# Where the second RMSNorm's scale is applied in a hybrid attention layer on one Trainium2 core

## Chip, core and metric

The kernel runs on one NeuronCore of a Trainium2 chip. Its engines run beside each other and meet only at semaphores: PE (TensorE, products into PSUM), DVE (VectorE), ACT (ScalarE), POOL (GpSimd) and SP (SyncE, which issues the loads). The metric is the device time of one execution in microseconds (us). All times below are us unless ns stands there.

## What is computed

One inference step of a one-layer encoder over 1024 prompt tokens and 64 sample tokens, 1088 columns in all, with 1024 channels. After the two attention branches comes the part that matters here:

```
x  = x + gt1 * einsum(merged, w_out)                      # output projection
h2 = rms_norm(x, g_norm2) * (1.0 + sc2) + sh2             # second norm, scale and shift per channel
u  = relu(einsum(h2, w_up))                               # 1024 -> 4096
x  = x + gt2 * einsum(u * u, w_down)                      # 4096 -> 1024
rms_norm(x, g) = x / sqrt(mean over channels of x*x + EPS) * g
```

gt1, sc2, sh2 and gt2 come from a conditioning vector: one value per channel for the prompt and one for the sample tokens. They lie in modT; gain2 is g_norm2 * (1 + sc2).

## The kernel before

Everything is kept transposed: channels in the partitions (KT = 8 tiles of 128), tokens in the columns. xT is x, 8 tiles of 1088 columns. A product with a float32 weight tile is made in three products of a rounded format: the high part of the weights with the high part of the data, high with low, low with high. So each operand is split into hi and lo: hi is a copy into the rounded type, lo the difference.

A job is one weight tile of 128 x 1024, loaded by SP into w_raw, split by POOL into w_hi (L724) and w_lo (L726), in two slots. POOL starts a split once PE has begun the job before it (w_used, L795) and the data has landed. PE runs group_product (L781) for three groups of 364, 362 and 362 columns (GROUPS, L35), each 8 channel tiles times three products, 24 in all, into a PSUM bank of its own; six banks are used in turn, and PE waits (bank_free, L786) until DVE has evicted the group six before. All three groups of a job use the same weights.

The output projection (L1162) is eight jobs, one for each tile m of xT. DVE adds each group, times gt1, to xT (add_scaled, L1881, L1892); ACT squares the finished tile into sq_tmp (L1457), DVE adds that to sq_sum (L1904). These are loops of four turns over two tiles.

Then comes the norm. PE waits for sq_sum and for all banks (L1170 to L1172), sums over the channels with nine pairs of products against a column of ones, tokens in the partitions (L1175). DVE makes the mean, ACT the root, DVE the reciprocal, of nine columns (L1909 to L1914). PE spreads the result over 128 partitions with nine pairs of products (L1182) into banks 5 to 7. Then for each of eight tiles: DVE multiplies xT by it (h2_n, L1927), ACT applies gain2 and the shift in two pieces, prompt and sample (h2_f, L1467), and copies to h2_hi (L1471), and the difference h2_lo is made by DVE for even tiles (L1919) and by POOL for odd ones (L769). The split of the first up job stands before these on POOL's queue, the second behind them.

The feed-forward is a loop of eight passes (L1191). A pass is four up jobs (d = 0 to 3) and four down jobs. In the very first group PE waits for h2_hi and h2_lo tile by tile (h2_ready, L1186). Each up group is evicted by DVE with relu (L1937), squared by ACT (L1479), copied to u_hi (L1481), and DVE makes u_lo (L1942), which waits for ACT before DVE goes to the next group. The first three groups of the down product wait for the last u_lo's (L1202). Down groups are added to xT by add_scaled (L1948). After the loop the final norm and the stores follow.

## Time and profile before

| | |
|---|---|
| median of 3 runs | 1935.29 (1929.22 to 1940.74) |
| the profiled execution: time | 1928.07 |
| its span, first to last instruction | 1926.3 |
| mean granted TensorE clock | 0.972 |
| output projection, last product starts | 1093.68 |
| first up job starts its second group | 1133.21 |
| second up job starts | 1142.21 |
| passes of the feed-forward | 8, from about 1132 to 1901 |

The profile is of one execution. Its first part gives busy time by engine. The chain of waits follows the work that ended last back from the end. The timeline gives instructions in order of time, with the idle time of their engine before them in brackets and what ended it; "x2" is two instructions merged in a row. The windows give busy time and the granted clock in a stretch, as a share of 2.4 GHz. The groups by form give count, total and mean duration of instructions of one line and shape. The trace names tiles by prefix: h_hi and h_lo stand for h2_hi and h2_lo there, h_n and h_f for h2_n and h2_f.

### The profile page before, as it was taken

The numbers are of one execution on the slowest core, as the hardware profiler recorded it, in microseconds if no ns is written. First come the engines' busy times: TensorE is split into PE (matmuls) and PEld (weight loads), VectorE is DVE, ScalarE is ACT, GpSimd is POOL, SyncE is SP. The second block draws the span as 40 slices with busy tenths as digits, with TensorE's granted clock in tenths as the row PEclk, the third lists the DMA queues.
The fourth block names the chain that finished last, engine by engine and source line by source line (L and its number), as shares of the span: only waits on it lengthen the run. The fifth ranks groups of instructions, "written<-read, shape, count | busy, mean of one in ns | idle before, by whom it ended". The sixth has DMA issues, their size and how long they took to land.

```text
span 1926.3 us, 30314 instructions
## 1 busy us (share of the span) xinstructions
PE 1811.3 (94%) x11206; PEld 1718.9 (89%) x11206; DVE 978.2 (51%) x2263; ACT 584.7 (30%) x1115; POOL 473.9 (25%) x273
## 2 busy tenths in 40 slices
PE   7599999999978898999999869999999999999996
PEld 2498999999978887778999869999999999999996
DVE  1547888899145556555653344343434343434344
ACT  3345566641244444443320151111111111111112
POOL 0331222224210100120323132222222222222220
PEclk9699999999989998999999979999999999999998
DMA  7420124242442223653443101111111111111112
GB/s 269 136 61 23 57 90 112 91 127 79 125 108 69 58 57 91 181 154 124 136 138 99 33 22 45 44 44 44 44 44 44 44 44 44 44 44 44 44 44 93
DMA packets 179317, 153.40 MB, mean 80 GB/s; under 512 B 20240, under 2 KB 162016, under 8 KB 178688
## 3 DMA queue, kind: packets, MB, share of 16 engines
q1 hardware_dynamic: 175328, 137.31, 24.8%
q10 hardware_dynamic: 3920, 15.19, 2.0%
q8 instruction: 42, 0.69, 0.2%
q14 instruction: 27, 0.22, 0.0%
HBM read 127.34 MB, written 25.19 MB: 79 GB/s over the span
## 4 chain that ended last, share of the span: by engine, by line
PE 83%; DVE 7%; ACT 5%; DMA 2%; issue 2%; POOL 1%; SPq 0%; DVEq 0%; ACTq 0%; POOLq 0%
PE psum L791 65%; PE psum L1066 4%; PE psum L1057 2%; PE psum L915 2%; PE psum L1084 2%; PE psum L948 2%; PE psum L829 1%; PE psum L1029 1%; PE psum L1030 1%; DVE u_lo L1942 1%; DVE h_f L1559 1%; PE psum L1033 1%; DVE logit L1754 1%; DMA out<-y_out 1%; DVE score L1616 1%
## 5 line engine op out<-in xcount | busy, mean ns | idle before, releaser
L791 PE MATMUL psum<-h_hi,w_hi 128*128 128x362 f32 (+1 forms) x1440 | 477.6, 332 | 17.5 <-POOL h_lo L769 10.7
L791 PE MATMUL psum<-h_lo,w_hi 128*128 128x362 f32 (+1 forms) x1440 | 475.6, 330 | 0.0
L791 PE MATMUL psum<-h_hi,w_lo 128*128 128x362 f32 (+1 forms) x1440 | 474.7, 330 | 0.0
L724 POOL CAST w_hi<-w_raw 128x1024 fp32r<-128x1024 f32 x112 | 124.5, 1112 | 1020.4 <-PEq L795 825.0
L791 PEld LDWEIGHTS psum<-h_hi,w_hi 128*128 128x128 f32 x1440 | 272.6, 189 | 21.4 <-POOL h_lo L769 12.6
L726 POOL TENSOR_TENSOR w_lo<-w_raw,w_hi 128x1024 fp32r<-128x1024 f32 x112 | 275.9, 2464 | 9.0
L1892 DVE SCALAR_TENSOR_TENSOR xT<-psum,modT,xT 128x64 f32<-128x64 f32 (+7 forms) x288 | 136.3, 497 | 275.3 <-PE psum L791 275.3
L791 PEld LDWEIGHTS psum<-h_hi,w_lo 128*128 128x128 f32 x1440 | 273.1, 190 | 0.0
L791 PEld LDWEIGHTS psum<-h_lo,w_hi 128*128 128x128 f32 x1440 | 273.0, 190 | 0.0
L791 PE MATMUL psum<-u_hi,w_hi 128*128 128x362 f32 (+1 forms) x768 | 253.2, 330 | 2.7 <-DVE u_lo L1942 2.7
L791 PE MATMUL psum<-u_lo,w_hi 128*128 128x362 f32 (+1 forms) x768 | 252.4, 329 | 0.0
L791 PE MATMUL psum<-u_hi,w_lo 128*128 128x362 f32 (+1 forms) x768 | 251.7, 328 | 0.0
L1479 ACT ACTIVATE u_sq<-u_relu 128x362 f32<-128x362 f32 (+1 forms) x96 | 48.8, 508 | 623.5 <-DVE u_relu L1937 623.5
L1942 DVE TENSOR_TENSOR u_lo<-u_sq,u_hi 128x362 fp32r<-128x362 f32 (+1 forms) x96 | 114.5, 1193 | 107.0 <-ACT u_hi L1481 107.0
L791 PEld LDWEIGHTS psum<-u_hi,w_hi 128*128 128x128 f32 x768 | 144.3, 188 | 5.1 <-issue 5.1
L791 PEld LDWEIGHTS psum<-u_hi,w_lo 128*128 128x128 f32 x768 | 144.7, 188 | 0.0
L791 PEld LDWEIGHTS psum<-u_lo,w_hi 128*128 128x128 f32 x768 | 144.5, 188 | 0.0
L1637 DVE TENSOR_SCALAR_CACHE_REDUCE count_dump<-score,thresh 128x384 f32<-128x384 f32 (+4 forms) x160 | 130.6, 876 | 1.1
L1937 DVE TENSOR_SCALAR u_relu<-psum 128x362 f32<-128x362 f32 (+1 forms) x96 | 51.2, 533 | 142.4 <-PE psum L791 142.4
L752 POOL TENSOR_TENSOR q_hl<-q_raw,q_hl 64x1088 fp32r<-64x1088 f32 x16 | 39.9, 2494 | 309.7 <-ACT q_hl L1372 285.7
L1292 ACT ACTIVATE sign_dump<-score,thresh 128x1024 f32<-128x1024 f32 x64 | 102.2, 1600 | 20.5 <-DVE thresh L1633 20.5
L1066 PEld LDWEIGHTS psum<-kv_tok,probT 128*128 128x128 f32 (+1 forms) x584 | 71.8, 196 | 18.4 <-issue 16.8
(286 smaller groups left out, 2813.8 us busy)
## 6 DMA issues: line engine op xcount, KB each, us to landing
w_raw<-in_w_in SPq DMA_DIRECT2D x32, 512.0 KB, 4.1
ada_c<-in_w_ada SPq DMA_DIRECT2D x32, 512.0 KB, 4.1
w_raw<-in_w_up SPq DMA_DIRECT2D x32, 512.0 KB, 4.0
w_raw<-in_w_down SPq DMA_DIRECT2D x32, 512.0 KB, 3.5
zT_scratch<-z_out ACTq DMA_DIRECT2D x27, 544.0 KB, 2.7
q_raw<-zT_scratch SPq DMA_DIRECT2D x32, 272.0 KB, 5.1
gate<-zT_scratch SPq DMA_DIRECT2D x16, 544.0 KB, 4.5
ada_w<-in_w_ada SPq DMA_DIRECT2D x4, 2048.0 KB, 9.6
```

Of the source, the lines that this page charges most:

```text
L724: pl.tensor_copy(w_hi[slot][:, :], w_raw[slot][:, :]).then_inc(sem("w_hi_made"), 1)
L726: pl.tensor_tensor(w_lo[slot][:, :], w_raw[slot][:, :], w_hi[slot][:, :].bitcast(F32), ALU.subtract).then_inc(sem("w_split"), 1)
L752: pl.tensor_tensor(q[64:P, :], q_raw[64:P, ::-1], q[64:P, :].bitcast(F32), ALU.subtract)\
L791: ins = pe.matmul(bank(b, n), w[:, k, wc], x[:, a, c0:c0 + n], start=(m == 0 and p == 0), stop=(m == len(wk) - 1 and p == 2))
L915: ins = pe.matmul(bank(4 + g, m), w[slot][:, k * P:k * P + P], x[:, k, c0:c0 + m], start=(k == 0 and p == 0), stop=(k == KT - 1 and p == 2))
L1066: ins = pe.matmul(bank(6 + u["n"] % 2)[:, HD * lane:HD * lane + HD], probT[s][0:n, m * P:m * P + P], values(u, kb), start=(kb == 0), stop= ...
L1292: ins = ac.activation(sign_dump[g % 2][r, 0:c.stop - c.start], score[r, c], ACT.Sign, scale=-1.0, bias=thresh[r, g:g + 1].bitcast(F32), ac ...
L1479: ac.activation(u_sq[:, s, 0:n], u_relu[:, s, 0:n], ACT.Square).then_inc(sem("u_squared"), 1)
L1637: return dv.tensor_scalar(count_dump[r, c], score[r, c], th[r, g:g + 1].bitcast(F32), None, op, ALU.add, accum_out=count[r, g:g + 1])
L1892: ins = dv.scalar_tensor_tensor(x, ps if isinstance(m, int) else ps.unsqueeze(1), gt, x, ALU.mult, ALU.add)
L1937: dv.tensor_scalar(u_relu[:, s, 0:n], bank(3 * (d % 2) + g, n), 0.0, None, ALU.max)\
L1942: dv.tensor_tensor(u_lo[:, d, c0:c0 + n], u_sq[:, s, 0:n], u_hi[:, d, c0:c0 + n].bitcast(F32), ALU.subtract).then_inc(sem("u_done"), 1)
```

## The change

h2 = rstd * (gain2 * x) + shift, and rstd is a number per token, so it can be applied after the product over channels: W_up h2 = rstd * (W_up (gain2 x)) + W_up shift. The changed kernel does this.

- In the output projection, ACT makes h2_hi of tile m as a copy of xT times gain2, in two pieces, and DVE makes h2_lo as xT times gain2 minus h2_hi, in two pieces, right after the tile's last group is evicted. The square and the sum follow. The loops are written out over eight tiles.
- h2_hi and h2_lo get two more columns at the front, the shifts of the prompt and of the sample. The up product runs over 1090 columns in groups of 366, 362 and 362 (UP_GROUPS). The two extra results are copied to b_up at the eviction.
- The norm's small steps and the pass over eight tiles go. In their place, after the second group of the first up job, three fp32 products of a 128x128 block of ones with sq_sum, over 512, 512 and 64 columns (spread_mean), give the sum in all partitions at once; the third waits until DVE has read both before it. DVE makes the mean, ACT the root, DVE the reciprocal of all 1088 columns (rstd_b).
- At the eviction of an up group DVE multiplies by rstd_b; ACT applies relu with b_up as bias (two pieces in the third group, where prompt and sample meet), then square and copy. DVE makes u_lo of a group behind the eviction of the next.
- POOL only splits weights. The first pass of the feed-forward is written out, and a loop of seven follows.

```diff
+UP_GROUPS = [(0, 366), (366, 362), (728, 362)]
+MEAN_PARTS = [(0, 512), (512, 512), (1024, 64)]
...
-        h2_hi = at("h2_hi", [P, KT, TOK], F32R, A)
-        h2_lo = at("h2_lo", [P, KT, TOK], F32R, A + ACTW)
+        h2_hi = at("h2_hi", [P, KT, TOK + 2], F32R, A)
+        h2_lo = at("h2_lo", [P, KT, TOK + 2], F32R, A + KT * (TOK + 2))
...
@@ GpSimd
-            split(0)
-            for k in range(1, KT, 2):
-                pl.wait_ge(sem("h2_hi_done"), k + 1)
-                pl.tensor_tensor(h2_lo[:, k, :], h2_f[:, k % 2, :], h2_hi[:, k, :].bitcast(F32), ALU.subtract)\
-                    .then_inc(sem("h2_done1"), 1)
-            for d in range(1, 8):
-                split(d % 2)
-            splits(7, 8)
+            splits(8, 8)
...
@@ TensorE
+            def spread_mean():
+
+                pe.wait_ge(sem("sq_added"), 1 + KT)
+                pe.wait_ge(sem("ones_ready"), 1)
+                for m, (c0, n) in enumerate(MEAN_PARTS):
+                    if m == 2:
+                        pe.wait_ge(sem("sq_mean"), 2)
+                    pe.matmul(bank(6 + m % 2, n), ones[:, :], sq_sum[:, c0:c0 + n], start=True, stop=True)\
+                        .then_inc(sem("sq_spread"), 1)
 
             def h2_ready(k):
-                pe.wait_ge(sem(f"h2_done{k % 2}"), k // 2 + 1)
+                pe.wait_ge(sem("h2_lo_done"), k + 2)
...
+                    for g, (c0, n) in enumerate(UP_GROUPS):
                         group_product(d % 2, KT, range(KT), slice(0, P), h2_hi, h2_lo, range(KT), c0, n, 3 * (d % 2) + g,
-                                      first=(g == 0), ready=h2_ready if d == 0 and g == 0 else None)
+                                      first=(g == 0), ready=h2_ready if first and d == 0 and g == 0 else None)
+                        if first and d == 0 and g == 1:
+                            spread_mean()
...
@@ ScalarE
+            for m in range(KT):
+                ac.wait_ge(sem("bank_free"), sums.next(3))
...
+                ac.activation(h2_hi[:, m, 2:2 + SEQ], xT[:, m, 0:SEQ], ACT.Copy, scale=gain2[:, m, 0:1])
+                ac.activation(h2_hi[:, m, 2 + SEQ:2 + TOK], xT[:, m, SEQ:TOK], ACT.Copy, scale=gain2[:, m, 1:2])\
+                    .then_inc(sem("h2_hi_done"), 1)
+                ac.wait_ge(sem("sq_added"), m + 1)
+                ac.activation(sq_tmp[:, :], xT[:, m, :], ACT.Square).then_inc(sem("squared"), 1)
...
-                        ac.wait_ge(sem("u_relu_done"), us.next())
+                        ac.wait_ge(sem("u_scaled"), us.next())
+                        for a, w, smp in seq_spans(g):
+                            x = u_relu[:, s, a - c0:a - c0 + w]
+                            ins = ac.activation(x, x, ACT.Relu, bias=b_up[:, d % 2, smp:smp + 1])
+                        ins.then_inc(sem("u_relu_done"), 1)
+                        ac.wait_ge(sem("u_relu_done"), us.n)
...
@@ VectorE
+                dv.wait_ge(sem("h2_hi_done"), m + 2)
+                dv.scalar_tensor_tensor(h2_lo[:, m, 2:2 + SEQ], xT[:, m, 0:SEQ], gain2[:, m, 0:1],
+                                        h2_hi[:, m, 2:2 + SEQ].bitcast(F32), ALU.mult, ALU.subtract)
...
+            for m, (c0, n) in enumerate(MEAN_PARTS):
+                dv.wait_ge(sem("sq_spread"), m + 1)
+                dv.tensor_scalar(rstd_b[:, c0:c0 + n], bank(6 + m % 2, n), 1.0 / DM, EPS, ALU.mult, ALU.add).then_inc(sem("sq_mean"), 1)
+            for m, (c0, n) in enumerate(MEAN_PARTS):
+                dv.wait_ge(sem("sq_root"), m + 1)
+                ins = dv.reciprocal(rstd_b[:, c0:c0 + n], rstd_b[:, c0:c0 + n])
...
-                        dv.tensor_scalar(u_relu[:, s, 0:n], bank(3 * (d % 2) + g, n), 0.0, None, ALU.max)\
-                            .then_inc(sem("u_relu_done"), 1)
...
+                        if g == 0:
+                            dv.tensor_copy(b_up[:, d % 2, :], ps[:, 0:2])
+                            ps = ps[:, 2:n + 2]
+                        dv.tensor_tensor(u_relu[:, k % 2, 0:n], ps, rstd_b[:, c0:c0 + n], ALU.mult).then_inc(sem("u_scaled"), 1)
+                        dv.wait_ge(sem("u_scaled"), relus.n + (k + 1))
                         dv.sem_inc(sem("bank_free"), 1)
+                        if k:
+                            u_low(k - 1)
+                u_low(11)
```

## Rows read from the trace of the kernel before

**Rows 1.** The page's first part: engine, busy us (share), instructions.

```profile
PE 1811.3 (94%) x11206; PEld 1718.9 (89%) x11206; DVE 978.2 (51%) x2263; ACT 584.7 (30%) x1115; POOL 473.9 (25%) x273
```

**Rows 2.** The chain of waits, 1097 to 1178: start, us, what.

```profile
1097.90 3.52 PE psum L1175 x18
1102.30 4.41 PE psum L1182 x18
...
1132.14 46.13 PE psum L791 x267
```

**Rows 3.** Timeline at the output projection's end: start, us, engine, line, instruction [idle before].

```profile
1093.68 0.32 PE L791 MATMUL psum<-m_hi,w_lo 128*128 128x362 f32 x1
1094.16 0.72 DVE L1892 SCALAR_TENSOR_TENSOR xT<-psum,modT,xT 128x298 f32 x2 [3.40 <-PE psum L791]
1095.08 1.11 ACT L1457 ACTIVATE sq_tmp<-xT 128x1088 f32 x1 [10.83 <-DVE xT L1892]
...
1096.31 1.29 DVE L1904 TENSOR_TENSOR sq_sum<-sq_sum,sq_tmp 128x1088 f32<-128x1088 f32 x1 [1.43 <-ACT sq_tmp L1457]
```

**Rows 4.** Timeline where the second up job starts, and POOL's next cast.

```profile
1142.21 0.33 PE L791 MATMUL psum<-h_hi,w_hi 128*128 128x364 f32 x1
...
1142.63 1.04 POOL L724 CAST w_hi<-w_raw 128x1024 fp32r<-128x1024 f32 x1 [7.10 <-issue]
1143.75 2.40 POOL L726 TENSOR_TENSOR w_lo<-w_raw,w_hi 128x1024 fp32r<-128x1024 f32 x1
1154.59 1.04 POOL L724 CAST w_hi<-w_raw 128x1024 fp32r<-128x1024 f32 x1 [8.44 <-issue]
```

**Rows 5.** Windows: stretch, us, busy by engine, granted clock, DMA share, GB/s.

```profile
1134.00:1136.00 2.00, 2.00 (x9) 2.00 (x8) 0.81 (x1) 1.01 (x2) 1.52 (x1) 0.54 0.00 0
```

**Rows 6.** Timeline: a sum begun inside POOL's w_lo, and ACT's two-piece scale.

```profile
1083.42 2.41 POOL L726 TENSOR_TENSOR w_lo<-w_raw,w_hi 128x1024 fp32r<-128x1024 f32 x1
1084.37 2.61 DVE L1904 TENSOR_TENSOR sq_sum<-sq_sum,sq_tmp 128x1088 f32<-128x1088 f32 x1 [1.44 <-ACT sq_tmp L1457]
...
1108.06 1.57 ACT L1467 ACTIVATE h_f<-h_n,modT,gain 128x1024 f32<-128x1024 f32 x2 [6.07 <-DVE h_n L1927]
```

**Rows 7.** Timeline of PE at the kernel's start: eight fp32 products of 512 columns.

```profile
29.23 7.03 PE L829 MATMUL psum<-ada_w,siluT 128*2 128x512 f32 x16
```

**Rows 8.** Timelines by engine where a pass turns from up to down.

```profile
1274.53 0.54 DVE L1937 TENSOR_SCALAR u_relu<-psum 128x362 f32<-128x362 f32 x1 [1.81 <-PE psum L791]
1276.17 2.50 DVE L1942 TENSOR_TENSOR u_lo<-u_sq,u_hi 128x362 fp32r<-128x362 f32 x1 [1.11 <-ACT u_hi L1481]
...
1275.64 0.51 ACT L1481 ACTIVATE u_hi<-u_sq 128x362 fp32r<-128x362 f32 x1
...
1275.87 2.41 POOL L726 TENSOR_TENSOR w_lo<-w_raw,w_hi 128x1024 fp32r<-128x1024 f32 x1
...
1278.80 0.43 PE L791 MATMUL psum<-u_hi,w_hi 128*128 128x362 f32 x1 [0.34 <-DVE u_lo L1942]
```

**Rows 9.** Groups by form, DVE's reciprocals: count | busy us, mean ns | idle before.

```profile
L1725 DVE RECIPROCAL rden<-rsum 128x1 f32<-128x1 f32 x36 | 5.7, 158 | 0.0
...
L1913 DVE RECIPROCAL mid_rstd<-mid_rstd 128x8 f32<-128x8 f32 x1 | 0.2, 202 | 0.4 <-ACT mid_rstd L1461 0.4
...
L1914 DVE RECIPROCAL mid_rstd<-mid_rstd 64x1 f32<-64x1 f32 x1 | 0.1, 103 | 0.0
```

**Rows 10.** Two gaps of PE in the attention part, and the windows around them.

```profile
537.11 0.77 PE L1057 MATMUL psum<-ident,logit 128*128 128x128 f32 x5 [2.41 <-ACT logit L1380]
...
605.92 0.55 PE L1057 MATMUL psum<-ident,logit 128*128 128x128 f32 x3 [1.59 <-DVE yA_lo L1789]
...
536.00:540.00 4.00, 2.89 (x15) 2.67 (x16) 1.05 (x2) 2.18 (x6) 0.73 (x3) 0.81 0.93 222
540.00:544.00 4.00, 4.00 (x24) 3.78 (x23) 2.32 (x7) 2.00 (x4) 0.00 (x0) 0.76 0.97 210
...
604.00:608.00 4.00, 2.41 (x23) 2.17 (x21) 2.00 (x8) 1.64 (x4) 0.00 (x0) 1.00 0.02 4
```

134 lines of the change are left out of this document (49 added, 85 removed).

## The prediction, made before the changed kernel was run

> **What bounds the kernel now.** I read the page's totals first: TensorE (PE) is busy 94% of the span [rows 1], so only a stretch where PE is not dense can give time back. The chain of waits names the one in reach [rows 2]: PE runs densely until 1094.0, then the chain passes through the two fp32 PE steps of the mean (L1175, L1182), VectorE (DVE), ScalarE (ACT) and GpSimd (POOL), and PE is dense again only from 1132.14. The timeline gives the ends: the last product of the output projection starts at 1093.68 and lasts 0.32 [rows 3]; the second job of the up product starts at 1142.21 [rows 4]. Between these lie three groups of 24 products. Jobs of three groups recur every 11.96 us (the casts of w_hi at 1142.63 and 1154.59, [rows 4]), or 0.166 us a product. So 1142.21 - 1094.01 = 48.2 us are spent on 12.0 us of work: the norm costs 36.2 us. Part of it is the clock: PE was idle from 1094.0 to 1097.9, and at 1134 it still ran mostly at the lower of its two levels, 1.2 GHz (0.54 granted, [rows 5]).
>
> **What goes.** Everything between the last eviction and the first up product: 3.5 us and 4.4 us of PE [rows 2], the small DVE and ACT steps, and eight tiles of h2_n, h2_f, h2_hi, h2_lo. POOL's share of h2_lo, every second tile, goes with them.
>
> **What stays on the path: tile 7.** Tiles 0 to 6 are split behind earlier products. The last tile is complete only with the eviction that starts at 1094.16 and takes 0.72 [rows 3]. ACT then makes h2_hi in two pieces, 1024 and 64 columns; the nearest row is the same pair with a bias, 1.57 together [rows 6]. Before, ACT started its square at 1095.08 [rows 3], so h2_hi is ready near 1095.08 + 1.57 = 1096.65. DVE then subtracts, both inputs in SBUF. Such a subtraction or sum takes 1.29 for 1088 columns when alone [rows 3], but 2.61 when it starts inside POOL's w_lo: started 1084.37, POOL busy 1083.42 to 1085.83, done 1086.98, 1.15 after POOL [rows 6]. Will POOL be there? It splits a job's weights once PE has begun the job before: cast 0.42 after the start, w_lo 1.12 later, 2.40 long [rows 4]. With the up product starting at 1094.05 that is 1095.6 to 1098.0, over the 1096.65. So h2_lo is ready at 1098.0 + 1.3 = 1099.3 (two pieces). PE meanwhile does 21 products of group 0, to 1094.05 + 21 x 0.166 = 1097.5, waits 1.8 us, and finishes the group with three at 1099.9. Bounds of this wait: 0.6 if POOL doesn't hold DVE, 3 if ACT and DVE are slower by 1.2 together. Group 1 ends at 1103.9.
>
> **Added on PE: the spread mean.** Three fp32 products with a 128x128 block of ones, 512, 512 and 64 columns. Nothing like it is in the trace. The nearest is 512 columns with two weight columns: 16 instructions, two to a product, in 7.03 us, 0.88 each product [rows 7]; a load of 128 fp32 weight columns adds a little, so I take 1.0. The third must wait until DVE has read the second: an eviction of 362 columns takes 0.54 [rows 8], so 0.7 for 512, with 0.3 for two hand-overs. Third product 0.3. Sum 1.0 + 1.0 + 0.7 + 0.3 + 0.3 = 3.3 us; bounds 2.1 (two bare products, the rest overlapped) and 5. It is all on the path, as group 2 is queued behind it.
>
> **Behind it, hidden.** DVE now takes the root's reciprocal over 1088 columns and not 9. Of the column counts in the trace, 8 take 202 ns and 1 takes 158 [rows 9], so 6.3 ns a column and 1088 x 6.3 = 6.9 us; with the 103 ns row as base it would be 14 ns and 15.4 us. What is queued behind it on DVE is the evictions of the first groups, and PE waits for those when it comes back to their banks. Spread done 1107.2, reciprocals from 1107.4 to 1114.3 (1122.8 at the upper bound). PE first asks for a bank not yet evicted at the third job, 1107.2 + 4.0 + 12.0 = 1123.2. So it costs nothing.
> The backlog then drains at ACT's rate: relu, square and copy, three times 0.51 [rows 8] or about 1.9 a group with hand-overs, against 4 us on PE. It is gone within four groups.
>
> **Added in the output projection.** Per tile, ACT gets 1.6 us and DVE about 1.4 plus a wait for ACT of 1.6 and a hold by POOL; behind that wait are queued the evictions of the next tile. Worst order after a tile's last group: 0.9 evictions, 1.6 ACT, held to 3.9, 1.4, then the sum 1.3, done at 6.6 us of the 12 us that a tile lasts. PE comes back to a bank six groups, 24 us, later. Nothing on the path. POOL and SP: the first two splits of the up product move forward with PE, their weights were loaded ahead (SP's waits are unchanged until g_fin).
>
> **Added in every up product: two columns and a longer eviction.** Two more columns in one group of three: 8 x 4 x 24 = 768 products by at most 2/364 of 0.166 us, 0.7 us; lower bound 0. The eviction is now a multiply by rstd (PSUM source, still 0.54), then relu on ACT, up to two spans, then square, copy, subtract. It matters once in each of eight passes, where the third group of the down product waits for the last u_lo. Now: eviction 1274.53, u_lo issued at 1276.17 but ended only at 1278.67, since POOL's w_lo runs 1275.87 to 1278.28; PE lost 0.34 [rows 8]. After: relu on 298 and 64 columns adds at most two times the 0.51 that 362 columns take, so u_lo is issued by 1277.2, still inside POOL's stretch, and ends at the same 1278.67. Cost 0; the cover is POOL's w_lo, with 1.1 us of it left. If relu needed over 2.1 us, each further us would cost 8. The other lower u_lo's leave POOL's way, since they are taken one group later. That brings DVE relief, no time.
>
> **The sum.** Second job starts after at 1094.05 + 12.0 + 1.8 + 3.3 = 1111.2, not 1142.2: -31.0. Two columns: +0.6. Net -30.4 us. The profiled execution has a span of 1926.3 and took 1928.07, so it would take 1897.7. But that execution is 7.2 us below the median of the three runs (1929.22 to 1940.74), and I take the median as the level: 1935.3 - 30.4 = 1904.9.
>
> **Rivals.**
> (a) The clock falls. PE now idles twice, 1.8 us and about 1.0 us, within 8 us. In the trace a gap of 1.59 us left the clock at 1.00 and one of 2.41 us was followed by 0.81 and 0.76 over two stretches of 4 us [rows 10]. Mine lie between. Price by these rows: (0.19 + 0.24) x 4 = 1.7 us, if PE is dense; with a spread mean at half speed 2 more. Result about 1908. Chance 0.2. The page "TensorE: Matmul & The Clock Gate" of the Trainium skill (A second HAM failure mode: psum-queue depth-cycling) speaks for it: small idle gaps between groups of products can make the clock swing. By that rule the time is this rival's.
> (b) The reciprocal becomes the bound. Decides above 1123.2 - 1107.4 = 15.8 us, 14.5 ns a column; each us beyond costs one. At 20 ns it is 6 us, 1911. The upper bound of [rows 9], 15.4 us, falls just short, and a hold by POOL could add the rest. Chance 0.07. The page "VectorE: DVE Perf Modes" of the Trainium skill (The DVE is not a fixed-function vector unit) says that a reciprocal runs an iterative divide with a repeat count of 8; at the 0.96 GHz it gives, that is an estimate of 9.1 us by this page, with which (b) would be as good as excluded.
> (c) The pace of the products changes. h2's rows become 1090 columns long and the groups start at 366 and 728, so moving reads shift by 8 bytes. This is the one mechanism that would make the kernel slower: 8 x 4 x 72 = 2304 up products, so it turns above 30.4/2304 = 13 ns a product (8%), and at 20 ns it adds 46 us, so 1904.9 + 46 = 1951. Against it: today's groups start at 364 and 726, one a multiple of 16 bytes and one not, in jobs that all last 11.96 [rows 4]. Chance 0.03; of a small change of pace, under 3 ns either way (7 us), 0.08.
> (d) The change doesn't do what it says: PE is still gated by something else of the gap, say h2_lo of several tiles done late since DVE is behind. Each late tile costs at most the 36.2 / 8 = 4.5 us that it costs now; with three it is 1918. Needs DVE at over 12 us a tile, the working above gives 7. Chance 0.03.
>
> **How the numbers follow.** Forecast 0.59, (a) 0.2, (b) 0.07, (c) 0.03 and 0.08, (d) 0.03. The forecast's own terms: wait 0.6 to 3, spread 2.1 to 5, columns 0 to 0.7: -28 to -33. The level of the runs moves by 6 either way. The range of 1893 to 1914 takes in the forecast, (a), most of (b) and the small change of pace. A measurement of this kernel can tell about 0.5%, 9.7 us, from no change: faster by more 0.94, within 0.03, slower by more 0.03.
>
> **What would show it.** In the changed trace: products dense to 1094, 21 of the up product at once, one gap near 1.8 us released by DVE's h2_lo, which is about 2.6 long for its first piece because of POOL; two fp32 products of 1.0 and a gap of 1.0 before the third; the second job at 1111 or so; granted clock 1.00 throughout; reciprocals of 3 to 5 us each, with no PE gap at the third job; u_lo before the down product still ending with POOL's w_lo, and PE gaps there of 0.34. Wrong if the clock row falls at 1100, if jobs of the up product last other than 11.96 + 0.02, or if the eight gaps grow.

## The result and the profile after

The kernel after took 1911.35 us (median of 4 runs, 1908.37 to 1917.14) beside 1935.82 for the kernel before on the same chip: a ratio of 0.9894, 95% interval 0.9871 to 0.9917. Two more comparisons later gave 0.9877 (0.9848 to 0.9906) and 0.9845 (0.9825 to 0.9866). By these ratios that is 20.5, 23.8 and 30.0 us, by the differences of the medians 24.5, 24.3 and 31.1 us. The forecast was 30.4: the direction was right, and the size was too large in two of the three comparisons. The profiled execution took 1911.76 us and has a span of 1909.8.

The chain of waits after, over the stretch of [rows 2] (start, length, what). Where the chain of before needed 38 us from the last dense product to the next one, this one needs 13, of which 4.78 are products:

```profile
1103.24 1.15 ACT h_hi L1457
...
1104.70 2.54 issue
1107.24 0.28 DVE h_lo L1905
...
1107.57 4.78 PE psum L788 x27
1112.35 1.73 PE psum L1174 x4
...
1114.10 0.70 DVE rstd_b L1914
...
1114.85 0.43 PE psum L1174 x2
1115.28 24.82 PE psum L788 x148
```

The same stretch in the timelines by engine, the counterpart of [rows 3, 4, 6, 9] (in brackets the idle time before the instruction and what ended it):

```profile
1102.12 0.33 PE L788 MATMUL psum<-m_hi,w_lo 128*128 128x362 f32 x1
...
1107.57 0.44 PE L788 MATMUL psum<-h_hi,w_hi 128*128 128x366 f32 x1 [1.59 <-DVE h_lo L1905]
...
1112.18 1.88 PE L1174 MATMUL psum<-sq_sum,ones 128*128 128x512 f32 x4
...
1104.66 2.65 DVE L1903 SCALAR_TENSOR_TENSOR h_lo<-xT,gain,h_hi 128x1024 fp32r<-128x1024 f32 x1 [1.46 <-ACT h_hi L1458]
...
1115.46 6.97 DVE L1917 RECIPROCAL rstd_b<-rstd_b 128x512 f32<-128x512 f32 x3
...
1103.84 2.40 POOL L731 TENSOR_TENSOR w_lo<-w_raw,w_hi 128x1024 fp32r<-128x1024 f32 x1
1119.60 1.04 POOL L729 CAST w_hi<-w_raw 128x1024 fp32r<-128x1024 f32 x1 [13.37 <-PEq L792]
```

The last product of the output projection starts at 1102.12, ending the projection's column at 1102.46. The second up job's cast starts at 1119.60, 17.14 us later; before it was 1142.63 - 1094.02 = 48.61 us [rows 4]. The norm's stretch has thus given 31.5 us, as forecast (31.0). It holds the whole norm and the first up job.

Three measures of the trace say where some of it went again. From the output projection's end to VectorE's last step for y_out (the output) the kernel before takes 827.62 us and the kernel after 802.64: 25.0 less and not 31.5. A pass takes 96.87 us instead of 96.25; from the second up job's cast to the first step behind the eight passes (L1212 in both kernels) it is 763.37 us (1119.60 to 1882.97) and not 758.57 (1142.63 to 1901.20), 4.8 more. And from there to the last y_out it is 22.13 us and not 20.44, 1.7 more (0.9 and 1.5 in the two later profiles of the kernel after). 31.5 - 4.8 - 1.7 = 25.0. In the profiled executions the rest of the difference lies ahead of the output projection, in the attention part, which the change doesn't touch (the first experiment). The chain at the end of before, then of after:

```profile
1901.20 1.11 PE psum L1212 x8
...
1921.64 1.27 DVE y_out L1967
...
1882.97 1.11 PE psum L1212 x8
...
1905.10 1.28 DVE y_out L1968
```

A pass is best seen in the chain, by its longest run of products with no gap (552 of them, from the third group of the first down job to the next turn). The first line is the kernel before, the second after: 0.46 us more in each; the other 0.16 are at the turn, where a pass goes from its up jobs to its down jobs.

```profile
1760.05 91.95 PE psum L791 x552
...
1741.08 92.41 PE psum L788 x552
```

### The profile page after: what moved, and what is told of

Its sections match the earlier page's. It is cut to its first block, busy times and chain, and to the rows that moved or that the text cites. A ratio compares the mean times of both kernels' runs of the same rounds, so it can differ in the third digit from the quotient of the medians.

```text
span 1909.8 us, 30260 instructions
## 1 busy us (share of the span) xinstructions
PE 1814.1 (95%) x11176; PEld 1722.1 (90%) x11176; DVE 947.0 (50%) x2302; ACT 638.8 (33%) x1237; POOL 470.0 (25%) x269
## 4 chain that ended last, share of the span: by engine, by line
PE 84%; DVE 6%; ACT 4%; DMA 3%; issue 2%; POOL 1%; SPq 0%; DVEq 0%; ACTq 0%; POOLq 0%
PE psum L788 65%; PE psum L1063 5%; PE psum L1054 3%; PE psum L912 2%; PE psum L1081 2%; PE psum L945 2%; PE psum L1026 1%; PE psum L826 1%; PE psum L1027 1%; DVE h_f L1557 1%; DMA ada_c<-in_w_ada 1%; PE psum L1030 1%; DVE u_lo L1927 1%; DMA out<-y_out 1%; DVE score L1614 1%
## 5 line engine op out<-in xcount | busy, mean ns | idle before, releaser
L788 PE MATMUL psum<-h_hi,w_hi 128*128 128x362 f32 (+2 forms) x1440 | 474.6, 330 | 2.5 <-DVE h_lo L1905 1.6
L788 PE MATMUL psum<-h_lo,w_hi 128*128 128x362 f32 (+2 forms) x1440 | 474.1, 329 | 0.0
L788 PE MATMUL psum<-h_hi,w_lo 128*128 128x362 f32 (+2 forms) x1440 | 473.5, 329 | 0.0
L731 POOL TENSOR_TENSOR w_lo<-w_raw,w_hi 128x1024 fp32r<-128x1024 f32 x112 | 281.7, 2515 | 9.0
L1889 DVE SCALAR_TENSOR_TENSOR xT<-psum,modT,xT 128x364 f32<-128x364 f32 (+3 forms) x288 | 136.1, 497 | 265.3 <-PE psum L788 265.3
L1474 ACT ACTIVATE u_relu<-u_relu,b_up 128x364 f32<-128x364 f32 (+3 forms) x128 | 63.5, 519 | 553.5 <-DVE u_relu L1939 553.5
L1939 DVE TENSOR_TENSOR u_relu<-psum,rstd_b 128x362 f32<-128x362 f32 (+1 forms) x96 | 51.1, 532 | 171.1 <-PE psum L788 171.1
L1063 PEld LDWEIGHTS psum<-kv_tok,probT 128*128 128x128 f32 (+1 forms) x584 | 77.0, 207 | 15.1 <-issue 13.5
L1063 PE MATMUL psum<-kv_tok,probT 128*128 128x64 f32 (+1 forms) x584 | 79.9, 290 | 10.4 <-ACT probT L1395 8.0
```

Source lines behind the costliest of these rows:

```text
L731: pl.tensor_tensor(w_lo[slot][:, :], w_raw[slot][:, :], w_hi[slot][:, :].bitcast(F32), ALU.subtract).then_inc(sem("w_split"), 1)
L788: ins = pe.matmul(bank(b, n), w[:, k, wc], x[:, a, c0:c0 + n], start=(m == 0 and p == 0), stop=(m == len(wk) - 1 and p == 2))
L1063: ins = pe.matmul(bank(6 + u["n"] % 2)[:, HD * lane:HD * lane + HD], probT[s][0:n, m * P:m * P + P], values(u, kb), start=(kb == 0), stop= ...
L1474: ins = ac.activation(x, x, ACT.Relu, bias=b_up[:, d % 2, smp:smp + 1])
L1889: ins = dv.scalar_tensor_tensor(x, ps if isinstance(m, int) else ps.unsqueeze(1), gt, x, ALU.mult, ALU.add)
L1939: dv.tensor_tensor(u_relu[:, k % 2, 0:n], ps, rstd_b[:, c0:c0 + n], ALU.mult).then_inc(sem("u_scaled"), 1)
```

## The experiments

Two theories stood at the outset. **Theory 1**: the difference between forecast and result lies in the level of single executions, that is the attention part's clock. **Theory 2**: the changed part itself gives some of the gain back in each pass, by the products' pace (rival (c) of the prediction in its small form) or by the turn. Both turned out to be at work.

### The level: the same kernels once more

after_again and after_third are the kernel after, before_again the kernel before, all unaltered.

> The changed kernel once more, unaltered, in five rounds beside the one before. Question: the profiles show three differences, -31.3 us between the output projection's end and the second up job, +0.62 us in each of eight passes, and +8.3 us in the attention part, which the change doesn't touch and where the granted clock fell twice in the changed kernel's profile (0.50 from 608 to 620 and from 668 to 676) and not in that of before. Theory 1 (the attention part's time varies from execution to execution with the clock, whatever the kernel): this profile again has 16.9 us for the norm's stretch and 96.87 us a pass, but another length of the attention part, anywhere from 357 to 366 us between 545 and the output projection, going with the clock in it; the median difference comes near -31.3 + 5.0 = -26 us, ratio 0.986 to 0.988. Theory 2 (the change makes the attention part slower, by other addresses or instruction fetch): again the clock falls there, +8 us, and the ratio is 0.990 to 0.992.

> The kernel before, unaltered, profiled once more. What is asked is whether the attention part of the kernel before also changes its length from one execution to the next, as that of the kernel after did (its output projection's end at 1102.46, 1098.33 and, in three near copies, about 1094 to 1096), or whether the change brings something fixed there. Theory 1 (the length goes with the clock granted in the attention part, by the execution): the start of the mix stage lies somewhere between 902 and 911 us, and not at 902.62 again but by chance; if it is above 904, some stretches after the gap before 606 us show a granted clock under 0.9. Theory 2 (the change brings it): 902.6 within 0.5 us again. Both expect the same from there on: the second up job 48.2 us after the output projection's end, 96.25 us a pass, and a turn from up to down of 2.48 us for the second group. A third question lies in the last microseconds: the second of the last writes of y_out before took 2.66 us and after 4.1 to 4.9; if that is the change's, it takes 2.7 here again.

> The kernel after, unaltered, once more, as the comparison on this chip for the combination. Expected from its two profiles so far: 801.9 to 802.6 us from the output projection's end to the last step of VectorE for y_out, a pass of 96.87 us, and a time between 1902 and 1912 by the length of the attention part; ratio to the kernel before 0.987 to 0.989.

The products that merge the two attention branches, with the output projection right behind them, started at 902.62 (before), 910.54 (before_again), 911.05 (after), 906.76 (after_again) and 900.41 us (after_third): one kernel alone varies by 10.6 us. So either kernel has early and late executions: theory 1 holds, and what looked like 8.4 us lost to the change in the first pair of profiles was not its doing. Windows of 4 us in before, after and before_again, in this order, each behind the same gap of 1.59 us (columns: window, length, busy time and instructions of TensorE, its weight loads, VectorE, ScalarE and GpSimd, then the granted clock, the DMA share and GB/s):

```profile
608.00:612.00 4.00, 3.02 (x28) 2.79 (x27) 1.69 (x4) 1.96 (x6) 0.00 (x0) 1.00 0.00 0
...
608.00:612.00 4.00, 3.44 (x16) 3.04 (x17) 0.98 (x2) 1.55 (x4) 0.00 (x0) 0.50 0.00 0
...
608.00:612.00 4.00, 3.44 (x17) 3.04 (x16) 0.98 (x2) 2.00 (x6) 0.00 (x0) 0.50 0.00 0
```

The gaps themselves, in after and before_again; that of before is in [rows 10]:

```profile
605.40 0.55 PE L1054 MATMUL psum<-ident,logit 128*128 128x128 f32 x3 [1.59 <-DVE yA_lo L1787]
...
605.86 0.55 PE L1057 MATMUL psum<-ident,logit 128*128 128x128 f32 x3 [1.59 <-DVE yA_lo L1789]
```

The same kernel, the same gap, and the clock is 1.00 in one execution and 0.50 (1.2 GHz) in another. Over the attention part from 545 to 900 us, the clocks were 0.98 in before, 0.94 in before_again and in after, and 0.98 in after_third. The stretch from the output projection's end to the last y_out step hardly varies: 827.62 and 828.39 for before; 802.64, 801.91 and 802.47 for after. The 0.77 of before_again lie in its norm: the second up job came 49.36 us behind the projection and not 48.61 (by the casts). These stretches, and no single time, are the measure for the experiments below; an effect of a few us can't be read from the medians. Most variants were run once, so each of their differences is that of one execution, though of eight passes in it.

### The norm's stretch: what holds tile 7, and can both stalls be hidden

pool_after_tile7 keeps GpSimd (POOL) away until tile 7 is split:

```diff
-            splits(8, 8)
+            split(0)
+            pl.wait_ge(sem("h2_lo_done"), KT + 1)
+            for d in range(1, 8):
+                split(d % 2)
+            splits(7, 8)
```

> The kernel after with GpSimd made to wait with the split of the second up job's weights until VectorE has written the low part of tile 7. Theory (GpSimd's subtraction holds VectorE at the port that the two share): the last piece's step on VectorE that took 2.65 us while GpSimd's ran falls to about 0.4 to 0.7, the gap of 1.59 us ahead of tile 7's products falls to 0.3 or less, and the second up job starts about 15.6 us after the output projection's end instead of 16.9 (down 1.3). Rival (the step of VectorE waits for ScalarE's rounding of tile 7 or for something else): the gap stays at 1.4 to 1.6 us and the start at 16.9. The split ends later by 2 to 4 us, which either theory takes as free: its product is wanted some 10 us later.

```profile
1100.59 1.28 DVE L1907 SCALAR_TENSOR_TENSOR h_lo<-xT,gain,h_hi 128x1024 fp32r<-128x1024 f32 x1 [1.46 <-ACT h_hi L1462]
...
1102.13 0.43 PE L792 MATMUL psum<-h_hi,w_hi 128*128 128x366 f32 x1 [0.22 <-DVE h_lo L1909]
1102.27 1.90 POOL L729 CAST w_hi<-w_raw 128x1024 fp32r<-128x1024 f32 x1 [12.01 <-DVE h_lo L1909]
```

VectorE's step takes 1.28 us and not 2.65, and the gap falls from 1.59 to 0.22. The third up job's cast came 27.82 us behind the projection's end instead of 29.19, 1.37 earlier. The hold by POOL's subtraction is shown. The expectation for the step itself, 0.4 to 0.7 us, was too low. (The cast's own start is no measure of the job here, since it now waits: 3.88 us behind the end and not 0.25.)

tile7_last orders the first up job by hand:

```diff
+                for part in (range(KT - 1), range(KT - 1, KT)):
+                    for g, (c0, n) in enumerate(UP_GROUPS):
...
+                        elif g:
+                            spread_mean(((0, 1), (2,))[g - 1])
```

> The kernel after with the first up job in another order: tiles 0 to 6 of all three groups of columns first, tile 7 of the three last, the ones product of the sum in its parts between them. Theory (both stalls of the first up job, 1.59 us ahead of tile 7 and 0.78 us for the bank of the third part of the sum, are waits for steps that work behind them would hide): both gaps under 0.2 us, and the second up job starts about 14.5 us after the output projection's end (from 16.9), between 14.2 and 15. The reciprocals still take about 7 us and stay hidden. Rival (the stalls only move: VectorE's squares and reciprocals now hold the first evictions, and banks come free late): the start is at 16 us or later, or a wait of over 0.5 us appears ahead of the second or the third up job. From there on nothing changes: 96.87 us a pass.

Its chain, the whole first up job, with tile 7's nine products of all groups at the end:

```profile
1096.36 7.04 PE psum L1197 x42
1103.40 1.72 PE psum L1176 x4
1105.11 3.52 PE psum L1197 x21
1108.63 0.17 PE psum L1176 x2
1108.80 1.55 PE psum L1197 x9
1110.35 14.72 PE psum L788 x88
```

There is no wait left in it: both stalls are hidden. The second up job's cast stands 14.25 us behind the projection's end instead of 17.14, and the whole stretch to the end takes 799.64, 2.3 us less than after_again.

### The turn from up to down

evict_as_before takes the longer eviction back (and so the product with 1/rms and the relu's shift out of the computation):

```diff
-                        dv.tensor_tensor(u_relu[:, k % 2, 0:n], ps, rstd_b[:, c0:c0 + n], ALU.mult).then_inc(sem("u_scaled"), 1)
+                        dv.tensor_scalar(u_relu[:, k % 2, 0:n], ps, 0.0, None, ALU.max).then_inc(sem("u_relu_done"), 1)
...
-                        ac.wait_ge(sem("u_scaled"), us.next())
-                        for a, w, smp in seq_spans(g):
-                            x = u_relu[:, s, a - c0:a - c0 + w]
-                            ins = ac.activation(x, x, ACT.Relu, bias=b_up[:, d % 2, smp:smp + 1])
-                        ins.then_inc(sem("u_relu_done"), 1)
-                        ac.wait_ge(sem("u_relu_done"), us.n)
+                        ac.wait_ge(sem("u_relu_done"), us.next())
```

> The kernel after with the eviction of the up product as it was: one maximum with zero on VectorE and no relu on ScalarE. Left out of the computation: the product with 1/rms and the shift, so the time is that of the rest. Theory A (the loss in the passes beyond the two columns comes from the longer eviction): the second group of the first down job falls from 2.63 to 2.48 us or below, as before, and the up jobs fall from 12.045 us towards 11.98; a pass falls from 96.87 to about 96.4. Theory B (the up jobs' pace comes from where the operands lie and from the two columns, the turn's loss alone from the eviction): the turn falls to 2.48, but the three up groups stay at 4.035, 4.016 and 3.995 us, and a pass takes 96.7. A third way: at the turn nothing changes either, because u_lo is still taken one group late and meets GpSimd's subtraction; then the turn stays at 2.6. The norm's stretch stays as it was, the second up job 17.1 us behind the output projection's end.

u_lo_at_once keeps the new eviction, but takes each u_lo right behind its own eviction and not one group late:

```diff
-                        if k:
-                            u_low(k - 1)
-                u_low(11)
+                        u_low(k)
```

> DVE makes u_lo of a group right after its eviction, as before the change, and not one group later. Theory: the turn from up to down loses time because DVE's u_lo of the second last group now holds the SBUF port when POOL's w_lo wants it, so POOL ends 0.15 us later and the last u_lo with it, and because that u_lo ends only as PE wants it. With u_lo at once the second last one is done 3 us earlier, POOL's w_lo lasts 2.41 and not 2.56, and a pass is 96.87 - 0.25 = 96.6 us. Rival (the longer chain over relu sets the turn): the pass stays at 96.87 or grows.

The turn in after, u_lo_at_once and evict_as_before, in this order (VectorE's, POOL's and TensorE's timelines; [rows 8] has it in before):

```profile
1253.00 0.97 DVE L1927 TENSOR_TENSOR u_lo<-u_sq,u_hi 128x362 fp32r<-128x362 f32 x1
1253.66 2.56 POOL L731 TENSOR_TENSOR w_lo<-w_raw,w_hi 128x1024 fp32r<-128x1024 f32 x1
...
1254.78 1.84 DVE L1927 TENSOR_TENSOR u_lo<-u_sq,u_hi 128x362 fp32r<-128x362 f32 x1 [0.81 <-ACT u_hi L1479]
...
1256.75 0.43 PE L788 MATMUL psum<-u_hi,w_hi 128*128 128x362 f32 x1 [0.40 <-DVE u_lo L1927]
...
1245.74 2.40 POOL L731 TENSOR_TENSOR w_lo<-w_raw,w_hi 128x1024 fp32r<-128x1024 f32 x1
...
1248.67 0.43 PE L788 MATMUL psum<-u_hi,w_hi 128*128 128x362 f32 x1 [0.31 <-DVE u_lo L1927]
...
1246.86 3.62 DVE L1922 TENSOR_TENSOR u_lo<-u_sq,u_hi 128x362 fp32r<-128x362 f32 x2
...
1247.52 2.56 POOL L731 TENSOR_TENSOR w_lo<-w_raw,w_hi 128x1024 fp32r<-128x1024 f32 x1
...
1250.60 0.43 PE L788 MATMUL psum<-u_hi,w_hi 128*128 128x362 f32 x1 [0.40 <-DVE u_lo L1922]
```

Without relu on ScalarE and without the multiply nothing moved: a pass of 96.87, the gap 0.40, the second group of the first down job 2.63 us (from the products' starts; 2.48 before the change). So theories A and B both fell as to the turn, and the expectation's third way held. What costs is the place of u_lo(10), the low part of the last group but one: taken behind the next eviction it runs from 1253.00 to 1253.97 across the start of POOL's w_lo at 1253.66, which then takes 2.56 and not 2.40 us, and the last u_lo ends with POOL. Taken at once, w_lo is 2.40 again, the gap 0.31, the group 2.46 and a pass 96.71. That is 0.16 us a pass and not the 0.25 expected. Eight times 0.16 would be 1.3, but the first pass went the other way (its second down group took 2.70 us and not 2.55), so that from the projection's end to L1212 the variant gained 1.0 (779.57 us against 780.5 to 780.6 in the three executions of the kernel after).

down_order doesn't shorten this wait but puts work ahead of it: both halves' products over u's first group of columns, then over the second, then over the third:

```diff
-                    for q in range(2):
-                        for g, (c0, n) in enumerate(GROUPS):
+                    for pos, (q, g) in enumerate(down_order(d)):
+                        c0, n = GROUPS[g]
...
+            return [(q, g) for g in range(3) for q in range(2)] if d == 0 else [(q, g) for q in range(2) for g in range(3)]
```

> The kernel after with the first down job of each pass in another order: the first group of columns for both halves of its outputs, then the second, then the third, so that products that need only the first group's u stand ahead of those that wait for the second's. Theory (the 0.6 us that each turn loses is a wait for the low part of the second group's u, which GpSimd's subtraction holds up): the gap is hidden; the first down job loses 0.56 to 0.6 us a pass, a pass takes 96.3 us instead of 96.87, eight passes give back 4.5 to 5 us. Rival (the loss is not in that wait but in the products' pace at the turn): the pass stays within 0.1 us of 96.87. A third way is that the order makes waits of its own, as banks come free in another order: a gap appears at the second down job of a pass, up to 0.5 us, and the pass gains less than 0.3 us.

Its six groups took 2.00, 2.00, 1.99, 2.00, 2.01 and 2.00 us (12.00 together, against 12.72 in after), and from the first up job's last group on, the chain names no wait in all of the feed-forward part, just one run:

```profile
1112.17 761.15 PE psum L792 x4560
```

The stretch to the end took 795.20 us, 6.7 less than after_again: 0.72 x 8 = 5.8 at the turns, which is over the 4.5 to 5 expected since the third group (2.10 before it) gained too, and about 1 at the writes of y_out, where the slow one now is the first.

### The pace of the products

Five kernels change where h2 lies and how many columns are read. layout_as_before and its two variants leave out the shift; plain_cols and shifts_last don't apply it either (relu's bias is zero in them).

```diff
layout_as_before:
-UP_GROUPS = [(0, 366), (366, 362), (728, 362)]
+UP_GROUPS = [(0, 364), (364, 362), (726, 362)]
-        h2_hi = at("h2_hi", [P, KT, TOK + 2], F32R, A)
+        h2_hi = at("h2_hi", [P, KT, TOK], F32R, A)
-        u_hi = at("u_hi", [P, 4, TOK], F32R, B + 32)
+        u_hi = at("u_hi", [P, 4, TOK], F32R, B)
two_more_columns, against layout_as_before:
-UP_GROUPS = [(0, 364), (364, 362), (726, 362)]
+UP_GROUPS = [(0, 366), (364, 362), (726, 362)]
rows_of_1090, against layout_as_before:
-        h2_hi = at("h2_hi", [P, KT, TOK], F32R, A)
+        h2_hi = at("h2_hi", [P, KT, TOK + 2], F32R, A)
-        u_hi = at("u_hi", [P, 4, TOK], F32R, B)
+        u_hi = at("u_hi", [P, 4, TOK], F32R, B + 32)
plain_cols, against after:
-UP_GROUPS = [(0, 366), (366, 362), (728, 362)]
+UP_GROUPS = [(2, 364), (366, 362), (728, 362)]
shifts_last, against after:
-UP_GROUPS = [(0, 366), (366, 362), (728, 362)]
+UP_GROUPS = [(0, 364), (364, 362), (726, 364)]
-        h2_hi = at("h2_hi", [P, KT, TOK + 2], F32R, A)
+        h2_hi = at("h2_hi", [P, KT, TOK + 8], F32R, A)
```

> The up product without the two shift columns: groups of 364, 362 and 362 columns from column 2 on, in the same tile with rows of 1090; b_up is set to zero once and the copy of the two columns at the eviction goes, so the shift is left out of the result. Tells what of the +0.085 us per up job is due to the number of columns. Theory count: up jobs fall from 12.05 to 11.97 us (11.96 before). Theory address (the groups start 8 bytes off and rows are 1090 long): they stay at 12.03 or more. The turn to the down product stays as in the changed kernel, 0.18 us longer than before.

> The up product with the two shift columns behind the tokens: groups of 364, 362 and 364 columns starting at 0, 364 and 726, as before the change, rows of 1096 columns, so every address is a multiple of the same powers of two as before. b_up is zero and its copy goes, so the shift is left out of the result. Theory count: up jobs stay near 12.05. Theory address: they go back to 11.96 + 0.02 = 11.98.

> The kernel after with the up product's operands laid out as before: rows of 1088 columns, groups of 364, 362 and 362 that start at 0, 364 and 726, and u_hi and u_lo at their old addresses. Left out of the computation: the shift. The eviction stays the long one of the change. Theory B (layout and columns set the pace): the three up groups return to 3.997, 3.963 and 4.000 us, the sum of an up job to 11.96, a pass takes 96.87 - 4 x 0.085 = 96.5 with the turn still at 2.63. Theory A (the eviction's traffic sets it): they stay within 0.01 of 4.006, 4.013 and 3.997, which is what the variant without the two columns but with rows of 1090 showed, and a pass stays at 96.76. Other down trios: 5.98 by theory B, 5.993 by A.

> The variant with the layout of before (rows of 1088, starts 0, 364, 726), but the first group's products read 366 columns instead of 364: two columns of the next group as well, which nobody uses. Left out of the computation: the shift. If the pace is set by the count of columns, only the first group changes, from 3.997 us to 4.02 (24 products by 0.9 ns), and the second and third stay at 3.962 and 3.977: up job 11.96. If it is not the count but the layout, all three stay as they were. By the prediction's term (two of 364 columns, 0.9 ns a product) the first group should be 4.018.

> The variant with the counts and starts of before (364, 362, 362 from 0, 364 and 726), but h2's rows 1090 columns apart, h2_lo moved behind accordingly and u_hi and u_lo 32 columns further, as the change has them. Left out of the computation: the shift. If the row pitch and the addresses set the pace, the second group rises from 3.962 towards 3.993 or more, the third from 3.977 to 3.995, and the other down trios from 5.971 to 5.993 us: an up job of 11.99 to 12.01. If the starts within the row set it, they stay at 3.997, 3.962 and 3.977, with only the down trios at 5.98 to 5.993.

Measured, from the starts of the products (mean of 12 jobs, good to about 0.003 us; the last column is the run of 552 in the chain):

| kernel | up group 1 | 2 | 3 | three other down groups | pass | run of 552 |
|---|---|---|---|---|---|---|
| before | 3.997 | 3.963 | 4.000 | 5.980 | 96.25 | 91.95 |
| layout_as_before | 3.997 | 3.962 | 3.977 | 5.971 | 96.12 to 96.42 | 91.46 to 91.98 |
| two_more_columns | 4.011 | 3.960 | 4.001 | 5.967 | 96.26 to 96.48 | 91.79 to 92.01 |
| rows_of_1090 | 3.992 | 4.010 | 3.987 | 5.993 | 96.57 to 96.65 | 92.11 to 92.19 |
| plain_cols | 4.006 | 4.013 | 3.997 | 5.993 | 96.76 | 92.30 |
| shifts_last | 4.000 | 3.993 | 4.018 | 5.980 | 96.60 | 92.14 |
| after | 4.035 | 4.016 | 3.995 | 5.993 | 96.87 | 92.41 |

Two of these runs in the chain, layout_as_before and rows_of_1090:

```profile
1247.21 91.95 PE psum L788 x552
...
1256.04 92.19 PE psum L788 x552
```

With the old layout the run is 91.95 again, to the last digit, in four of its seven runs (the others 91.98, 91.47 and 91.46), though the long eviction is still there; such a pass keeps only the 0.17 of the turn. And evict_as_before, with the short eviction and the new layout, kept 4.035, 4.017 and 3.994 us. So the pace belongs to layout and count (theory B). Step by step, by the steady passes: rows 1090 apart and u 32 columns further 0.23 us a pass; groups that start at 2, 366 and 728 and not at 0, 364 and 726 0.11; two more columns, with the first start back at 0, 0.11 (plain_cols to after). With the turn: 96.25 + 0.17 + 0.23 + 0.11 + 0.11 = 96.87. The direct test of the count, two_more_columns, is less clear: four of its runs took 92.01, 0.06 more than 91.95, and three took 91.79, less than without the columns. In it the two columns cost the first group 0.014 us and not the 0.021 of the forecast's rule.

Expectations that fell: in shifts_last and plain_cols the second group did not come back to 3.963; neither has rows of 1088. The expectation for shifts_last also took its addresses for multiples of the same powers of two as before, which they are not: 1088 is 64 x 17, its rows of 1096 are 8 x 137. Since layout_as_before is not wholly steady, its third group of 3.977, and with it the third group's rise to 4.001 in two_more_columns, is no finding, and why two of its runs took 91.46 stays open. Which of pitch and base address acts in rows_of_1090 was not separated.

### The last writes

In every profile of the kernel after and of its variants but the one below, one of the last writes of y_out takes 4.1 to 4.9 us, and in neither of before. (In layout_as_before, two_more_columns and rows_of_1090 another one takes 3.4.) The chain of before, then of after; behind them a line of after's DMA queues in the window 1891.97 to 1896.84 (packets, MB, share of the 16 DMA engines' time):

```profile
1910.52 2.66 DMA out<-y_out
...
1891.97 4.87 DMA out<-y_out
...
q8 instruction: 1, 0.02, 2.4%
```

One packet of code, 2.4% x 16 x 4.87 = 1.9 us of one DMA engine, lies in that window; in the windows of before's writes there is none. VectorE waits for the write to land before it may overwrite its buffer. pe_code_shift moves TensorE's code behind by 128 instructions:

```diff
             jobs = Count()
+            for _ in range(128):
+                pe.sem_inc(sem("pe_pad"), 1)
```

> The kernel after with 128 increments of an unused semaphore at the head of TensorE's program, where it waits for its first data anyway. They move all its code behind by 128 instructions and cost the time of nothing else. Asked is what makes one of the last writes of y_out take 4.1 to 4.9 us instead of 2.7 in every run of the kernel after and of its variants, and in none of the kernel before: in that write's window the trace shows one packet of code, of 16 KB, on queue q8. Theory (a load of TensorE's code falls on that write, since the first pass now stands outside the loop and the code is longer): the packet moves away from the end, all four of the last writes on the chain take 2.6 to 2.9, and from the transposes to the end it is 1.4 to 2.2 us less. Rival (q8 is another engine's, or the write is slow for a reason of its own): the second write stays at 4 to 5 us. Nothing else is expected to change by over 0.5 us, except that a code load can now fall elsewhere.

The same write in this kernel, and the price of the edit:

```profile
1900.97 2.68 DMA out<-y_out
...
5.36 15.28 issue
```

All writes on the chain take 2.67 to 2.71 again, and from the last turn's long run to the end it is 161.84 us instead of 163.2 to 164.0. No packet of q8 lies in its writes' windows. So the code load is the cause, as far as one execution shows it, and the engine is TensorE, as only its code was moved; the first pass now stands outside the loop, so that the code is longer. The expectation was wrong on the edit's own cost: TensorE's first product starts at 20.64 us and not at 5.58, so the 128 increments took 15 us, 0.12 us each, in a place where I had thought it waits for data anyway. The kernel took 1918.55 us.

### The edits together

all_three has tile7_last's order, down_order's and shifts_last's columns; like shifts_last it leaves out the shift in relu, and its eviction one small copy in each up job.

> The kernel after with three edits whose single runs gave time: the first up job with tile 7 last (second up job 14.25 us behind the output projection's end and not 17.14), the first down job of a pass by groups (2.00 us for each of its six), and the shift's two columns at the end of the rows (up job 12.01 us and not 12.045). Theory (they save in different places, so they add): from the output projection's end to the last write's VectorE step it is 801.9 - 2.9 - 8 x 0.58 - 8 x 0.27 = 792.2 us, with a range of 791 to 793.5 for where a code load falls on the writes of y_out; a pass takes 96.3 - 0.27 - about 0.05 = 96.0 to 96.1 us. Beside the kernel before, whose same stretch takes 827.6 to 828.4, that is 35.8 us less and a ratio of 1 - 35.8/1932 = 0.9815, where the kernel after has 0.988. Rival (they get into each other's way: a bank comes free late for the reordered down job when the up job is shorter, or tile 7's order meets the shift's columns): the stretch stays at 794 or more, with a gap on TensorE at a turn or at the second up job, and the ratio at 0.983 or above.

> The kernel after with two of the edits, all of the computation in place: the first up job with tile 7 last, and the first down job of a pass by groups. Theory (they add): second up job 14.25 us behind the output projection's end, 2.00 us for each of the six groups of the first down job and 96.29 us a pass; from the output projection's end to the last step of VectorE for y_out 801.9 - 2.9 - 8 x 0.58 = 794.4 us, with down_order's extra gain at the writes 792 to 793.5. The median 8 to 9.5 us below that of the kernel after on this chip, which is 0.45 to 0.5%, just what five rounds can tell; beside before a ratio of 0.983, with 0.9805 + 0.001 = 0.9815 as the end on the good side. Rival (they do not add): the stretch is 795 or more and the median within 5 us of the kernel after.

```diff
combined, against after: tile7_last's and down_order's diffs
all_three, against combined: shifts_last's diff
```

all_three took 1893.21 us (1891.86 to 1898.16, five runs), ratio 0.9805 (0.9777 to 0.9834), and 790.35 us from the projection's end on, 1.9 better than expected and outside the range given; a pass took 95.89 us (96.0 to 96.1 expected). combined computes everything. Its chain runs from the end of the first up job through all eight passes without one wait, with 96.14 us a pass:

```profile
1108.59 757.07 PE psum L792 x4536
```

The stretch takes 792.36 us against 802.47 in after_third, 10.1 less: the edits add. The median is 1900.92 us (1893.62 to 1905.29) against 1905.51 (1900.94 to 1910.92), ratio 0.9824 (0.9806 to 0.9843) against 0.9845 (0.9825 to 0.9866): 4.6 us less and not 8 to 9.5, with intervals that overlap. The trace shows the gain; the medians, with the attention part's clock in them, can't yet tell the two kernels apart.

## Why the prediction was wrong, and where it was right

**The step that failed: what the eight passes cost.** The sum gave them 0.6 us for the two columns, put the longer eviction at 0 and the place of the operands at nothing, and had no term for the end. The passes cost 4.8 us (763.37 against 758.57) and the end 0.9 to 1.7. The largest part is the place of h2 and u, 2.7 us, and the next the delayed u_lo, 1.3 at most; both are below. Two of the prediction's own signs of being wrong are in the trace: an up job lasts 12.05 us and not 11.98, and the eight gaps grew from 0.34 to 0.40. So of 31.5 us won in the norm's stretch 25.0 to 25.7 were left in the three profiles of the kernel after, beside the first one of before (827.62), and not 30.4.

**What bounded the kernel: right.** The gap behind the output projection was the place, and 31.5 us of it went (31.0 forecast). The output projection, with more work on ScalarE and VectorE beside it, kept its pace: with the merging products ahead of it it took 191.4 us in both first profiles (1102.46 - 911.05, before 1094.02 - 902.62), and its own 576 products took 95.8 in both.

**Tile 7: right, in mechanism and size.** The chain has one gap there, behind 21 products, and not several; rival (d) is out. h2_hi took 1.15 + 0.25 us (1.57 forecast), the subtraction 2.65 under POOL (2.61 in [rows 6]), the gap 1.59 (1.8). pool_after_tile7 shows the cause.

**Spread mean: right, slightly over.** 1.88 us for two products of 512 columns (1.0 each forecast), the eviction 0.69 (0.7), the last product 0.43; from 1112.18 to the next product 2.9 us against 3.3. tile7_last shows that it need not have had a wait in it.

**Reciprocals: right.** 6.97 us (6.9); 3.3 for 512 columns, 6.4 ns each. Hidden: the third up job came 12.05 us behind the second. Rival (b) is out. The estimate of 9.1 us by the repeat count of 8 that the page "VectorE: DVE Perf Modes" of the Trainium skill gives (in First, the fixed hardware budget, and not in the section that the prediction names) was too high; the measurement decides.

**The clock behind the norm, rival (a): did not come.** TensorE idled 1.59 and 0.78 us, and the granted clock stayed at 1.00 (2.4 GHz) in each window, one of which is:

```profile
1110.00:1114.00 4.00, 4.00 (x18) 2.75 (x17) 0.69 (x1) 0.03 (x1) 0.00 (x0) 1.00 0.00 1
```

But the argument for its chance fell: "a gap of 1.59 us left the clock at 1.00" was one execution's outcome and in others the same gap was followed by 0.50. What the page "TensorE: Matmul & The Clock Gate" of the Trainium skill says (A second HAM failure mode: psum-queue depth-cycling), that frequent small gaps between groups of products can make the clock swing, agrees with the attention part of after (1.00 until 604 us, 0.50 from 608 to 620, 0.95 behind that), and not with this stretch.

**The turn, "Cost 0": wrong.** The prediction saw that the last u_lo ends with POOL's w_lo and took POOL's end as fixed. It even named the edit that moved it, the low parts taken one group later, and judged "relief, no time". Delayed by one group, u_lo(10) meets the start of POOL's subtraction, and both get longer: 0.16 us a pass, 1.3 in all at most. Relu's own length was covered, as said: evict_as_before, without relu, has the same gap.

**Two columns: the count was right, the layout was not costed.** 0.11 us a pass or less, so at most 0.9 us for 0.6 forecast (the working gave 0.7). The rows' pitch with the moved addresses and the starts of groups cost 0.34 more, 2.7 us in eight passes, 1.2 ns for each up product: rival (c) in its small form, which had got a chance of 0.08. The argument against it (one start on a multiple of 16 bytes and one not, in jobs that all last 11.96) compared groups only as sums of a job. By group, before's own groups of 362 columns differ: 3.963 and 4.000 us. A look at the single groups would have shown that the place matters.

**The writes at the end: not in the sum.** The slow write took 1.4 to 2.2 us more through TensorE's longer code; since before's last write took 2.92 us and after's 2.67, the end as a whole lost 0.9 to 1.7. The diff showed the pass outside the loop, and the prediction didn't ask what longer code does.

**The level.** The median as the base was the right choice, but the start of the merging products moves by 7.9 us between two executions of before and by 10.6 between three of after, and three comparisons gave 20 to 30 us for a change that in the traces gives 25.0 to 26.5 (827.62 and 828.39 against 801.91 to 802.64). That the clock of the attention part moves it is read from the windows; nothing was changed to test it. So the sum should have read -31.5 + 4.8 (turn, place and columns, 0.62 us a pass, less the first up job's share, which the first term holds) + 0.9 to 1.7 = -25.0 to -25.8.

## What to carry to other kernels

A wait that "ends with another engine anyway" is a cover only as long as that engine's end doesn't move: follow each step that the change shifts to whatever shares a resource with it. Where a change touches the rows or starts of an operand that thousands of products read, time single groups and not whole jobs, and where it unrolls a loop ask where the code loads fall. Measure a small change in the stretch that it touches, beside the same stretch of the kernel before, since the same kernel's other parts can differ by more than the change from one execution to the next.

## What the runs showed of the hardware

- The same gap of 1.59 us of TensorE in the same kernel was followed by a granted clock of 1.00 in one execution and 0.50 in the next, and the end of the attention part differed by up to 10.6 us between executions of one kernel.
- VectorE and GpSimd hold each other both ways: VectorE's 1.28 us step took 2.65 in GpSimd's subtraction, and GpSimd's cast 1.90 us instead of 1.04 beside VectorE's sum (pool_after_tile7).
- The pace of otherwise equal products of 362 columns went from 3.96 to 4.01 us per 24 with the place of their operand (layout_as_before and rows_of_1090).
- A 512 KB write of 2.7 us took 4.1 to 4.9 where a packet of TensorE's code lay in its window, and 2.68 when that code was moved (pe_code_shift, one execution).
- An increment of a semaphore by TensorE took 0.12 us (15.1 us for 128, pe_code_shift).
